# Hgrn stage: gate, query and forget products as three rounded passes, the residual spilled to memory, and the mixing stage moved to mLSTM's end

## The chip, the cores and the metric

One Trainium2 chip, of which the kernel uses one core. The metric is the device time of one execution in microseconds (us); a median of several runs stands for a kernel. All arrays are float32.

## The reference, cut to what matters

Three blocks run one after the other on a sequence of 512 tokens of width 1024. The change touches two places, both here in short.

```python
# first block, mixer of layer 0 (HGRN): h is the normed input, hc the normed context of 256 tokens
q, v, zf, zb, gate = split(h @ w_in, 5)          # w_in: 1024 x 10240, 16 heads of 128
f = lb + (1 - lb) * sigmoid(z)                   # for zf and zb; g = log f, k = 1 - f
# per head and direction, with the context's state before it:
#   S_t = diag(exp g_t) S_{t-1} + k_t^T v_t ;  o_t = S_t^T silu(q_t)
y = (rmsnorm(o_forward + o_backward) * silu(gate)) @ w_out
x = x + gate_ada * y

# second block, three mixers side by side:
#   mLSTM (4 heads); gmlp: gelu(u) * (tril(ws) @ layer_norm(gelu(v)) + bs), 4 groups, chunks of 128 tokens;
#   attention with compressed keys: 31 windows of 32 tokens, phi(k) = gelu((window + pe) @ phi1) @ phi2, the same for v
```

## The kernel before, in words

The program is a row of stages. Each stage is a block of its own: every engine has its own instruction list in it, semaphores order them, and all engines meet at its end. Activations lie transposed in SBUF, `[128 partitions, 8 slices of the width, 512 tokens]`: `K.xT` is the residual stream, `K.hT` the normed input of a stage, `K.ctxT` the normed context.

`modulation_phase` (L255) streams 72 MB of matrices through six buffers; its loads are all issued by SyncE's queue (SP), and a norm stage follows it.

`hgrn_phase` (L439) loops over 16 heads. For each head, SP loads five weight tiles of 1024 x 128 (`W[m]` for V, ZF, ZB, Q, G; each load waits for the last product that used its buffer). TensorE runs `project(h)`: eight products in the order of `GROUPS`, namely V over the 512 tokens and over the context (L542), then ZF and ZB each over the 512 tokens and over the 256 tokens of the context, then Q and G over the 512 tokens (L548). A float32 product appears in the trace as two MATMUL records, so 16 records make one product of 1024 x 128 x 512. The products rotate through four PSUM banks, so product n waits until product n-4 has been read out. After `project(h)` TensorE runs `recur(h-1)`, the scores and states of the head before. In the middle of `project(h)`'s V product stands `mean_square(h-2)` (L529), the sum for the norm of head h-2.

ScalarE (ACT) works in a fixed order, `step(h)`: the logarithms of the forget gates of head h-1 (`logs`, L645), the exponentials of its forward direction (`exps`, L653 to L659), the read-out of V of head h, the exponentials of the backward direction, the read-out of ZF, ZB, Q and G (sigmoid and silu, L637, L639), then `recur(h-1)`, which ends with Ln and Exp of the mean square (L670, L672); that last pair waits for TensorE's `mean_square`, one head later. VectorE (DVE) finishes head h-2 (L779, L782), scales the gates of head h-1 (`f1`, L717, and `kk`, L721), scans them (L728, L729), forms differences (L735 to L743), and, when the exponentials are there, the products with q and k (L754 to L758). GpSimd (POOL) is idle in the loop.

Elsewhere in the kernel the large products are already done in three rounded passes: ACT copies a weight tile to the type fp32r (the high part, `WH`), POOL subtracts it from the original (the low part, `WL`), and TensorE adds high x high, high x low and low x high, one MATMUL record each (`product_phase`, L797; POOL's subtraction is L845, ACT's copy L877, TensorE's passes L861 to L863; in later stages L1877 and L2826 are such subtractions).

`mlstm_phase` (L1285) computes four heads and, between them, 16 side products (L1343), of which the last four run at its end. Its last head's norm is two products with a matrix of ones (L1380 mean, L1382 square). The stage after it, `mix_compress_phase` (L1503), loads its weights with 14 DMAs, transposes the gmlp matrices, does the gmlp mixing (L1545, and L1546 for the bias, 16 of each), the window products over 31 windows (L1555, 128 of 64 x 64 x 31), the same products for the position (L1561, one column each), and a small second layer. Then `attention_phase` starts.

Of the kernel before, what the change touches and what calls it, by code (L numbers as in the profile page):

```python
# [83 lines left out]
def constants_phase(K):  # L84
# [15 lines left out]
    K.tri = K.sb(K.ctx, "tri", [P, P])  # L100
    K.xT = K.sb(K.ctx, "xT", [P, KD, T])
    K.hT = K.sb(K.ctx, "hT", [P, KD, T])
# [152 lines left out]
def modulation_phase(K):  # L255
# [9 lines left out]
    with ExitStack() as st:  # L265
# [7 lines left out]
        summed, copied, turned, biased, zeroed, ready = sems[SLOTS:SLOTS + 6]  # L273
# [12 lines left out]

# [152 lines left out]
def hgrn_phase(K, hO):  # L439
# [12 lines left out]
    with ExitStack() as st:  # L452
        W = [K.sb(st, f"hg_w{m}", [P, KD, P]) for m in range(5)]
        vt = [K.sb(st, f"hg_v{i}", [P, NT // P, P]) for i in range(2)]
        sg = [[K.sb(st, f"hg_sig{i}{d}", [P, NT]) for d in range(2)] for i in range(2)]
        qs = [K.sb(st, f"hg_q{i}", [P, T]) for i in range(2)]
        gs = [K.sb(st, f"hg_gate{i}", [P, T]) for i in range(2)]
        f1 = [K.sb(st, f"hg_f{d}", [P, NT]) for d in range(2)]
# [14 lines left out]
        osq = K.sb(st, "hg_osq", [P, T])  # L473
# [3 lines left out]
        tmp = K.sb(st, "hg_tmp", [P, 32])  # L477
        tmp2 = K.sb(st, "hg_tmp2", [P, 32])
# [5 lines left out]
         at_ok, kv_ok, s_ok, out_ok, sq_ok, ms_ok, ln_ok, rs_ok, o1_ok, fin_ok, back_ok) = sems[5:31]  # L484

# [10 lines left out]
        with nc.Block() as block:  # L496
            @block.sync
            def _(sp):
                clear_old(sp, old)

                def load(h, first, shift=0):
                    at = h * P if first else sp.snap(h * P)
                    for m in (V, ZF, ZB, Q, G):
                        if not first:
# [3 lines left out]
                with sp.Fori(0, NH - 1) as before:  # L508
                    load(before, False, P)

# [13 lines left out]

            @block.tensor
            def _(pe):
# [4 lines left out]
                def project(h, p, first=False, owed=None):  # L531
                    for n, (m, c) in enumerate(GROUPS):
                        if c == 0:
                            pe.wait_ge(w_in[m], 16 * h + 16)
                        if n >= 4 or not first:
# [10 lines left out]
                        else:  # L546
# [76 lines left out]
            def _(act):  # L623
                act.wait_ge(f_ok, 1)
                act.activation(tmp2[:, :], tmp[:, :], ACT.Exp).then_inc(g_ok, 1)

                def evacuate(h, p, groups):
                    for n in groups:
                        m, c = GROUPS[n]
                        act.wait_ge(proj, NG * h + (n + 1))  # L630
                        bank = ps[n % 4]
# [3 lines left out]
                        elif m in (ZF, ZB):  # L635
                            s = sg[p][m - ZF]
# [37 lines left out]
                def step(h, p):  # L674

                    logs(h - 1)
# [6 lines left out]
                evacuate(0, 0, range(NG))  # L683
# [10 lines left out]
            def _(dve):  # L694
# [3 lines left out]
                dve.tensor_tensor(tmp[:, :], x, x, ALU.subtract).then_inc(f_ok, 1)  # L698
                dve.wait_ge(g_ok, 1)
                dve.reciprocal(lb[:, :], tmp2[:, :]).then_inc(lb_ok, 1)  # L700
                dve.wait_ge(lb_ok, 1)
                dve.tensor_tensor(tmp[:, :], tmp2[:, :], lb[:, :], ALU.mult).then_inc(lb_ok, 1)
                dve.wait_ge(lb_ok, 2)
                dve.tensor_tensor(lb[:, :], tmp[:, :], tmp[:, :], ALU.subtract).then_inc(lb_ok, 1)
                dve.wait_ge(lb_ok, 3)
                dve.tensor_scalar(omlb[:, :], lb[:, :], -1.0, 1.0, ALU.mult, ALU.add).then_inc(lb_ok, 1)
                dve.memset(ones_c[:, :], 1.0).then_inc(f_ok, 1)
                dve.wait_ge(lb_ok, 4)
# [5 lines left out]
                def prepare(h, p):  # L714
                    for d in range(2):
                        dve.wait_ge(evac, NG * h + 4 + 2 * d)
                        dve.tensor_scalar(f1[d][:, :], sg[p][d][:, :], omlb[:, bass.ds(h + NH * d, 1)], TINY,  # L717
# [567 lines left out]
def mlstm_phase(K, qk, mv, so, gu, nq, kvc, ksw, gate_rows, Pt_room, room):  # L1285


    nc = K.nc
    BM, NM, IB = gate_rows
    w = K.inp["w_in_2"][0].rearrange("(k p) n -> p k n", p=P)  # L1290
    WS = 6
    side = [(((MO + i * P, P),), so, i) for i in range(4)] + [(((GU + i * P, P),), gu, i) for i in range(4)]
    side += [(((NQ + i * DH, DH), (NQ + (i + 4) * DH, DH)), nq, i) for i in range(4)]
    side += [(((NKC + i * P, P),), kvc, i) for i in range(2)] + [(((NKS + 2 * i * P, P),), ksw, i) for i in range(2)]
# [10 lines left out]
    with ExitStack() as st:  # L1305
        Pt = Pt_room[:, :, :].rearrange("q (b j) t -> q b j t", b=2)
        D, floor, h, sq, rs = room[:, 0:2, :], room[:, 2:4, :], room[:, 4:6, :], room[:, 6, :], room[:, 7, :]
        W = [K.sb(st, f"ml_w{s}", [P, KD, P]) for s in range(WS)]
        ps = K.psum_banks(st, "ml")
        SIDE_BANK = (ps[6], ps[7])  # L1310
        sems, old = K.phase()
# [4 lines left out]
        with nc.Block() as block:  # L1316
            @block.sync
            def _(sp):
                clear_old(sp, old)
                for n, (pieces, _, _) in enumerate(side):  # L1320
# [3 lines left out]
                    for at, width in pieces:  # L1324
                        sp.dma_start(W[n % WS][:, :, to:to + width], w[:, :, at:at + width]).then_inc(w_in[n % WS], 16)
                        to += width

            @block.tensor
            def _(pe):
# [46 lines left out]
                def norms(a):  # L1376
# [3 lines left out]
                    pe.matmul(ps[1][:, :], K.ones[:, :], h[:, a % 2, :], start=True, stop=True).then_inc(mean, 1)  # L1380
                    pe.wait_ge(sqd, a + 1)
                    pe.matmul(ps[1][:, :], K.ones[:, :], sq, start=True, stop=True).then_inc(var, 1)  # L1382

                for s in range(MH + 2):
# [6 lines left out]
                    if s >= 2:  # L1391
                        if s >= 3:
                            pe.wait_ge(ln_ok, s - 2)
                        norms(s - 2)

            @block.scalar
            def _(act):
# [32 lines left out]
                for s in range(MH + 2):  # L1430
# [9 lines left out]
                    if s >= 2:  # L1440
# [3 lines left out]
                        norms(s - 2)  # L1444

# [55 lines left out]


def mix_compress_phase(K, vn, gu, kvc, kcmp, vcmp):  # L1503


    nc, inp = K.nc, K.inp
    names = (("nsa_phi_k1_2", "nsa_phi_k2_2", "nsa_pe_k_2"), ("nsa_phi_v1_2", "nsa_phi_v2_2", "nsa_pe_v_2"))
    with ExitStack() as st:
        ws = K.sb(st, "gm_w", [P, 4, P])
        wT = K.sb(st, "gm_wT", [P, 4, P])  # L1510
        bs = K.sb(st, "gm_bias", [1, 4, P])
        w1 = [K.sb(st, f"cp_w1{n}", [P, 32, DH]) for n in range(2)]
# [1697 lines left out]
```

## Time and profile before

| | |
|---|---|
| median of 3 runs | 4458.1 us (4453.8 to 4460.87) |
| the profiled execution | 4456.16 us, span 4454.4 us |
| TensorE busy | 3947.5 us (89%) |
| VectorE / ScalarE / GpSimd busy | 40% / 28% / 13% |
| granted TensorE clock over the span | 0.93 of full |
| DMA | 313.34 MB, mean 70 GB/s, at most 387 GB/s in one of 40 slices |

The granted clock has two levels, full (2.4 GHz) and half (1.2 GHz); 0.93 is the mean. The hgrn stage lies at about 262 to 1281 us of the span, mLSTM at 2144 to 2318, the mixing stage at 2318 to 2377. The busy share of TensorE is that of whole stages with different limits, so the stages are read one by one.

### The profile page before, as it was taken

The page shows a single profiled execution, that of the slowest core. Times are in us where ns is not written, and L with a number is a line of the kernel's source. Part 1 is how long each engine was busy: PE and PEld are TensorE (multiplying, and loading weights), DVE is VectorE, ACT ScalarE, POOL GpSimd, SP SyncE. Part 2 cuts the span into 40 slices and gives each one's busy share as a digit, 9 for nine tenths or more (in the row PEclk, how much of TensorE's full clock was granted, in tenths as well). Part 3 has the DMA queues.
Part 4 walks back from the last instruction along what each step waited for, and adds up shares of the span by engine and source line. Part 5 has one row for each costly group of instructions (what it writes and reads, how often), then busy time and mean ns, then how long its engine had stood idle before and what let it go on. Part 6 is the DMA issues. An engine that isn't in the chain of part 4 may idle for free. (4 is left out here: it accounts for less than half of the span.)

```text
span 4454.4 us, 57808 instructions
## 1 busy us (share of the span) xinstructions
PE 3947.5 (89%) x23667; PEld 2612.2 (59%) x23667; DVE 1795.5 (40%) x2993; ACT 1237.7 (28%) x2102; POOL 576.5 (13%) x302
## 2 busy tenths in 40 slices
PE   5789999999968997877889999999786777899998
PEld 2356666666655443334446554788555657687876
DVE  1023445444441999312222333433226537334421
ACT  0133343333332111222212322332323131323321
POOL 0000000000011000001000001344330020243442
PEclk7789999999979999988987999999898888999999
DMA  8921111111023221011221103333120010232331
GB/s 314 387 64 44 47 42 42 40 40 47 24 57 94 76 73 60 19 53 38 61 37 48 43 24 104 85 96 99 33 54 2 13 46 3 77 95 85 95 90 62
DMA packets 484578, 313.34 MB, mean 70 GB/s; under 512 B 28364, under 2 KB 441605, under 8 KB 484390
## 3 DMA queue, kind: packets, MB, share of 16 engines
q1 hardware_dynamic: 484390, 310.67, 23.5%
q8 instruction: 137, 2.24, 0.2%
q14 instruction: 51, 0.42, 0.0%
HBM read 308.54 MB, written 2.10 MB: 70 GB/s over the span
## 5 line engine op out<-in xcount | busy, mean ns | idle before, releaser
L548 PE MATMUL hg_bank<-hT,hg_w 128*128 128x512 f32 x1024 | 447.3, 592 | 0.0
L1009 PE MATMUL cv_bank<-hT,cv_w 128*128 128x512 f32 x768 | 334.0, 596 | 14.2 <-DMA cv_w<-in_conv_w_in_dram 14.2
L548 PEld LDWEIGHTS hg_bank<-hT,hg_w 128*128 128x128 f32 x1024 | 193.5, 190 | 223.5 <-issue 221.8
L1083 DVE SCALAR_TENSOR_TENSOR conv_u<-cv_pad,vec,conv_u 128x512 f32<-128x512 f32 x480 | 318.7, 748 | 0.0
L2826 POOL TENSOR_TENSOR tl_wl<-tl_w,tl_wh 128x1024 fp32r<-128x1024 f32 (+1 forms) x104 | 246.4, 2371 | 520.0 <-ACT tl_wh L2937 519.9
L1009 PEld LDWEIGHTS cv_bank<-hT,cv_w 128*128 128x128 f32 x768 | 146.9, 191 | 199.6 <-issue 184.6
L1877 POOL TENSOR_TENSOR mp_wl<-mp_w,mp_wh 128x1024 fp32r<-128x1024 f32 x72 | 173.3, 2409 | 598.7 <-ACT mp_wh L1957 598.7
L2937 ACT ACTIVATE tl_wh<-tl_w 128x1024 fp32r<-128x1024 f32 (+1 forms) x104 | 108.5, 1043 | 357.5 <-PE tl_bank L2863 355.3
L2861 PE MATMUL tl_bank<-tl_room,tl_wh 128*128 128x512 f32 x464 | 186.2, 401 | 12.8 <-POOL tl_wl L2826 12.0
L2863 PE MATMUL tl_bank<-tl_room,tl_wl 128*128 128x512 f32 x464 | 183.8, 396 | 0.0
L2862 PE MATMUL tl_bank<-tl_room,tl_wh 128*128 128x512 f32 x464 | 182.7, 394 | 0.0
L1665 PE MATMUL at_bank<-hT,at_w 128*128 128x512 f32 x384 | 176.7, 604 | 0.3 <-DMA at_w<-in_w_in_dram 0.3
L845 POOL TENSOR_TENSOR ho_wl<-ho_w,ho_wh 128x2048 fp32r<-128x2048 f32 x8 | 36.6, 4580 | 1070.9 <-ACT ho_wh L877 1070.9
L763 DVE COPY hg_probe<-hg_bank 128x1 f32<-128x1 f32 x32 | 5.1, 159 | 397.6 <-PE hg_bank L563 397.6
L1957 ACT ACTIVATE mp_wh<-mp_w 128x1024 fp32r<-128x1024 f32 x72 | 76.2, 1060 | 252.2 <-PE mp_bank L1897 244.5
L2861 PE MATMUL tl_bank<-tl_hh,tl_wh 128*128 128x512 f32 x352 | 139.4, 396 | 4.3 <-DVE tl_rest L3041 4.3
L2863 PE MATMUL tl_bank<-tl_hh,tl_wl 128*128 128x512 f32 x352 | 139.5, 396 | 0.0
L2862 PE MATMUL tl_bank<-tl_rest,tl_wh 128*128 128x512 f32 x352 | 139.3, 396 | 0.0
L542 PE MATMUL hg_bank<-hg_w,hT 128*128 128x128 f32 x1024 | 121.5, 278 | 16.4 <-DMA hg_w<-in_hgrn_w_in_dram 16.4
L542 PEld LDWEIGHTS hg_bank<-hg_w,hT 128*128 128x128 f32 x1024 | 119.5, 194 | 24.6 <-DMA hg_w<-in_hgrn_w_in_dram 16.8
L1895 PE MATMUL mp_bank<-mp_dh,mp_wh 128*128 128x512 f32 x320 | 129.0, 403 | 0.0
L1897 PE MATMUL mp_bank<-mp_dh,mp_wl 128*128 128x512 f32 x320 | 124.7, 390 | 0.0
(657 smaller groups left out, 7713.1 us busy)
## 6 DMA issues: line engine op xcount, KB each, us to landing
ada_w<-in_w_ada_dram SPq DMA_DIRECT2D x24, 2048.0 KB, 19.7
hg_w<-in_hgrn_w_in_dram SPq DMA_DIRECT2D x80, 512.0 KB, 3.8
mp_w<-in_w_mlp_dram SPq DMA_DIRECT2D x64, 512.0 KB, 4.1
ada_w<-in_ada_w_dram SPq DMA_DIRECT2D x12, 2048.0 KB, 19.9
cv_w<-in_conv_w_in_dram SPq DMA_DIRECT2D x48, 512.0 KB, 3.9
tl_w<-in_w_ffn_in_dram SPq DMA_DIRECT2D x44, 512.0 KB, 3.9
at_w<-in_w_in_dram SPq DMA_DIRECT2D x24, 512.0 KB, 4.0
tl_w<-in_w_in_dram SPq DMA_DIRECT2D x20, 512.0 KB, 3.9
```

What stands on the lines that cost most here:

```text
L542: ins = pe.matmul(bank[:, t * P:(t + 1) * P], src[:, k, t * P:(t + 1) * P], W[m][:, k, :], start=(k == 0), stop=(k == KD - 1))
L548: ins = pe.matmul(bank[:, 0:w], W[m][:, k, :], src[:, k, 0:w], start=(k == 0), stop=(k == KD - 1))
L1009: ins = pe.matmul(ps[n % RING][:, :], W[n % SLOTS][:, k * P:(k + 1) * P], K.hT[:, k, :], start=(k == 0), stop=(k == KD - 1))
L1083: ins = dve.scalar_tensor_tensor(o, x, by, o, ALU.mult, ALU.add)
L1665: ins = pe.matmul(SIDE_BANK[:, :], W[n % WS][:, k, :], K.hT[:, k, :], start=(k == 0), stop=(k == KD - 1))
L1877: pool.tensor_tensor(WL[u % SPLIT][:, :, :], W[(UPS + u) % RAW][:, :, :], WH[u % SPLIT][:, :, :].bitcast(F32), ALU.subtract).then_inc(low, 1)
L1895: pe.matmul(bank[:, :], wh[:, k, :], rh[:, k, :], start=(k == 0), stop=False)
L1897: ins = pe.matmul(bank[:, :], wl[:, k, :], rh[:, k, :], start=False, stop=(k == KD - 1))
L2826: pool.tensor_tensor(WL[u % SPLIT][:, 0:n, :], W[u % RAW][:, 0:n, :], WH[u % SPLIT][:, 0:n, :].bitcast(F32), ALU.subtract).then_inc(low, 1)
L2861: pe.matmul(to[:, :], wh[:, wk, :], rh[:, k, :], start=first, stop=False)
L2862: pe.matmul(to[:, :], wh[:, wk, :], rl[:, k, :], start=False, stop=False)
L2863: ins = pe.matmul(to[:, :], wl[:, wk, :], rh[:, k, :], start=False, stop=last)
```

## The change

Six things are changed.

1. In the hgrn stage the products of ZF, ZB, Q and G over the 512 tokens become three rounded passes. ACT makes `WH` and POOL makes `WL` for each of the four weight tiles of each head; there are two buffers of each, ZF and Q share one, ZB and G the other. V and the products over the context stay as they were.
2. The rounded input `hh` and its rest `hl` are made once at the stage's start (8 ACT copies, 8 DVE subtractions).
3. To make room, `hh` lies where the residual `K.xT` lay: SP writes `K.xT` (2 MB) to memory at the end of the modulation stage and waits for it, and reads it back in the last head.
4. Q and G share one weight buffer: G's load waits for the split of Q, and Q's load of the next head for the split of G.
5. Sigmoid's result goes straight into `f1`, scaled in place, and some small tiles share room (the square `osq` lies on `ATS`).
6. `mix_compress_phase` is dissolved into `mlstm_phase`: its loads stand behind the first six side loads, its window products between the last head's mean and square, the rest behind; the bias of the mixing is one product of 512 columns for each group instead of four of 128. The side products change order (the four query ones last).

```diff
 @@ modulation_phase, sync
+                sp.dma_start(K.spill, K.xT[:, :, :].rearrange("p k t -> p (k t)")).then_inc(spilled, 16)
+                sp.wait_ge(spilled, 16)
 @@ hgrn_phase
-        W = [K.sb(st, f"hg_w{m}", [P, KD, P]) for m in range(5)]
+        W = [K.sb(st, f"hg_w{m}", [P, KD, P]) for m in range(4)]
+        W.append(W[Q])
+        WH = [K.sb(st, f"hg_wh{m}", [P, KD, P], F32R) for m in range(2)]
+        WL = [K.sb(st, f"hg_wl{m}", [P, KD, P], F32R) for m in range(2)]
 @@ sync, load(h, first): h + 1 is loaded
                     for m in (V, ZF, ZB, Q, G):
-                        if not first:
+                        if m == G:
+                            sp.wait_ge(low, 3 if first else 4 * h + 7)
+                        elif m == Q and not first:
+                            sp.wait_ge(low, 4 * h + 4)
+                        elif not first:
                             sp.wait_ge(proj, NG * h + LAST_OF[m])
...
+                sp.wait_ge(proj, NG * NH)
+                sp.dma_start(K.xT[:, :, :].rearrange("p k t -> p (k t)"), K.spill).then_inc(x_back, 16)
+                sp.wait_ge(x_back, 16)
 @@ gpsimd
+                with pool.Fori(0, NH) as h:
+                    for j, m in enumerate((ZF, ZB, Q, G)):
+                        pool.wait_ge(high, 4 * h + (j + 1))
+                        pool.tensor_tensor(WL[j % 2][:, :, :], W[m][:, :, :], WH[j % 2][:, :, :].bitcast(F32), ALU.subtract).then_inc(low, 1)
 @@ tensor, project
-                        if c == 0:
+                        if m == V and c == 0:
                             pe.wait_ge(w_in[m], 16 * h + 16)
+                        elif c == 0:
+                            pe.wait_ge(low, 4 * h + m)
...
+                        else:
+                            wh, wl = WH[(m - 1) % 2], WL[(m - 1) % 2]
+                            for k in range(KD):
+                                pe.matmul(bank[:, :], wh[:, k, :], hh[:, k, :], start=(k == 0), stop=False)
+                                pe.matmul(bank[:, :], wh[:, k, :], hl[:, k, :], start=False, stop=False)
+                                ins = pe.matmul(bank[:, :], wl[:, k, :], hh[:, k, :], start=False, stop=(k == KD - 1))
 @@ scalar
+                def weights_high(h, m, first=False):
+                    act.wait_ge(w_in[m], 16 * h + 16)
+                    if m in (Q, G):
+                        act.wait_ge(proj, NG * h + (3 if m == Q else 5))
+                    elif not first:
+                        act.wait_ge(proj, NG * h - (1 if m == ZF else 0))
+                    act.activation(WH[(m - 1) % 2][:, :, :], W[m][:, :, :], ACT.Copy).then_inc(high, 1)
 @@ scalar, evacuate: after the read-out of ZF and of ZB over the 512 tokens
+                        if m in (ZF, ZB) and c == 0:
+                            weights_high(h, Q if m == ZF else G)
 @@ scalar, step(h)
+                    weights_high(h, ZF)
+                    weights_high(h, ZB)
                     logs(h - 1)
                     exps(h - 1, 0)
                     evacuate(h, p, range(0, 2))
                     exps(h - 1, 1)
                     evacuate(h, p, range(2, NG))
                     recur(h - 1)
 @@ mlstm_phase, tensor, end
+                    if a == MH - 1:
+                        windows()
                     pe.wait_ge(sqd, a + 1)
                     pe.matmul(ps[1][:, :], K.ones[:, :], sq, start=True, stop=True).then_inc(var, 1)
...
+                def mixes():
+                    pe.wait_ge(wt_ok, 1)
+                    pe.wait_ge(hq, 4 * MH)
+                    for x in range(4):
+                        for c in range(TT):
+                            pe.matmul(MIX[x][:, c * P:(c + 1) * P], vn[:, c, x * P:(x + 1) * P], wT[:, x, :],
+                                      start=(c == 0), stop=False, skip_group_check=True)
+                        pe.matmul(MIX[x][:, :], K.ones[0:1, :], bs[:, x, :].unsqueeze(1).broadcast_to((1, TT, P)),
+                                  start=False, stop=True, skip_group_check=True).then_inc(mixed, 1)
...
+                positions()
+                mixes()
+                compressed()
```

`windows()` begins with the transposes, which wait for the stage's loads and for the last side product's read-out; `positions()` waits for DVE's copy of the transposed positions, which DVE does after the last head's norm.

## Rows read from the trace of the kernel before

**Rows 1.** Windows of the hgrn stage: busy us of each engine, clock, DMA.

```profile
480.00:540.00 60.00, 59.31 (x405) 40.85 (x405) 28.11 (x55) 22.95 (x43) 0.00 (x0) 1.00 0.15 43
```

**Rows 2.** Timeline of TensorE, one head: start us, us, engine, line.

```profile
682.12 3.74 PE L542 MATMUL hg_bank<-hg_w,hT 128*128 128x128 f32 x32
...
693.70 7.03 PE L548 MATMUL hg_bank<-hT,hg_w 128*128 128x512 f32 x16
700.57 3.62 PE L548 MATMUL hg_bank<-ctxT,hg_w 128*128 128x256 f32 x16
...
728.08 0.49 PE L582 MATMUL hg_bank<-ident,hg_ks 128*128 128x128 f32 x3
```

**Rows 3.** Timeline of TensorE with rounded passes, first and last of 14 triples.

```profile
1320.42 0.39 PE L861 MATMUL ho_bank<-ho_rh,ho_wh 128*128 128x512 f32 x1
...
1329.94 0.39 PE L861 MATMUL ho_bank<-ho_rh,ho_wh 128*128 128x512 f32 x1
```

**Rows 4.** Timeline of ScalarE, the same head as rows 2.

```profile
687.48 0.63 ACT L672 ACTIVATE hg_ors<-hg_ors 128x512 f32<-128x512 f32 x1
...
697.07 1.95 ACT L653 ACTIVATE hg_lev<-hg_lev 128x256 f32<-128x256 f32 x6 [4.92 <-DVE hg_ks L743]
...
701.45 0.85 ACT L634 ACTIVATE hg_v<-hg_bank 128x512 f32<-128x512 f32 x2
...
708.05 0.87 ACT L637 ACTIVATE hg_sig<-hg_bank 128x512 f32<-128x512 f32 x2
```

**Rows 5.** Timeline of VectorE, the same head.

```profile
689.65 1.14 DVE L717 TENSOR_SCALAR hg_f<-hg_sig,hg_omlb 128x768 f32<-128x768 f32 x2
```

**Rows 6.** Timeline where VectorE and GpSimd meet, two places.

```profile
2093.78 2.34 POOL L845 TENSOR_TENSOR qk_wl<-qk_w,qk_wh 128x1024 fp32r<-128x1024 f32 x1 [10.85 <-ACT qk_wh L877]
2094.57 1.83 DVE L1272 TENSOR_SCALAR merge_gate<-qk_pad,vec 128x512 f32 x1 [2.48 <-ACT qk_pad L1265]
...
2755.16 0.68 DVE L2047 TENSOR_TENSOR mp_dl<-merge_gate,mp_dh 128x512 fp32r<-128x512 f32 x1
2755.57 2.50 POOL L1877 TENSOR_TENSOR mp_wl<-mp_w,mp_wh 128x1024 fp32r<-128x1024 f32 x1 [374.86 <-ACT mp_wh L1957]
2755.77 2.85 DVE L2064 TENSOR_TENSOR merge_gate<-merge_gate 128x512 f32<-128x512 f32 x1
```

**Rows 7.** DMA issues: count, KB each, median us to landing (whole span; 2140 to 2150).

```profile
hg_w<-in_hgrn_w_in_dram SPq DMA_DIRECT2D x80, 512.0 KB, 3.8
ml_w<-in_w_in_dram SPq DMA_DIRECT2D x4, 512.0 KB, 6.2
```

**Rows 8.** Timeline: four loads issued in a row, and the first's reader.

```profile
2073.34 4.04 SPq L835 DMA_DIRECT2D qk_w<-in_w_in_dram  x4
2077.06 1.06 ACT L877 ACTIVATE qk_wh<-qk_w 128x1024 fp32r<-128x1024 f32 x1 [1.58 <-DMA qk_w<-in_w_in_dram]
```

**Rows 9.** Timeline of the modulation stage's end.

```profile
227.76 3.64 PE L314 MATMUL ada_bank<-ada_w,ada_cond 128*32 128x512 f32 x16 [0.90 <-DMA ada_w<-in_w_ada_dram]
...
235.62 1.28 ACT L394 ACT_TABLE_LOAD   x1 [3.56 <-PEq L274]
```

**Rows 10.** Timeline from mLSTM's last norm to the attention stage.

```profile
2311.18 1.02 PE L1380 MATMUL ml_bank<-merge_gate,ones 128*128 128x512 f32 x2
2313.70 1.13 PE L1382 MATMUL ml_bank<-merge_gate,ones 128*128 128x512 f32 x2 [1.50 <-ACT merge_gate L1423]
2317.04 0.69 DVE L1492 TENSOR_TENSOR ml_o<-ml_o,merge_gate 128x512 f32<-128x512 f32 x1
...
2324.49 0.80 PE L1545 MATMUL gm_bank<-gm_wT,gm_v 128*128 128x128 f32 x2 [0.78 <-DVE gm_wT L1583]
...
2347.80 13.87 PE L1555 MATMUL gm_bank<-nsa_kvc,cp_w 64*64 64x31 f32 x256
...
2377.61 0.76 PE L1678 MATMUL at_bank<-nsa_ksw,nsa_q 64*128 64x128 f32 x2 [0.80 <-PEq L1523]
```

**Rows 11.** Timeline of TensorE: small products at the full clock.

```profile
3459.79 6.87 PE L2615 MATMUL rw_bank<-rw_E 64*64 64x64 f32 x229
```

More of the change, by code:

```diff
@@ L100, in constants_phase @@
     K.tri = K.sb(K.ctx, "tri", [P, P])
+    with ExitStack() as under:
+        K.hgH = K.sb(under, "hg_hh", [P, KD, T], F32R)
     K.xT = K.sb(K.ctx, "xT", [P, KD, T])
+    K.spill = nc.dram_tensor("x_spill", [P, KD * T], F32, kind="Internal").ap()
     K.hT = K.sb(K.ctx, "hT", [P, KD, T])
@@ L484, in hgrn_phase @@
          at_ok, kv_ok, s_ok, out_ok, sq_ok, ms_ok, ln_ok, rs_ok, o1_ok, fin_ok, back_ok) = sems[5:31]
+        high, low, h_high, h_low, x_back = (K.ctx.enter_context(nc.semaphore(f"hg_sem{n}")) for n in range(5))
         GROUPS = [(V, 0), (V, 1), (ZF, 0), (ZF, 1), (ZB, 0), (ZB, 1), (Q, 0), (G, 0)]
@@ L545, in project @@
                                     mean_square(owed)
-                        else:
+                        elif c == 1:
                             for k in range(KD):
@@ L630, in evacuate @@
                         act.wait_ge(proj, NG * h + (n + 1))
+                        if n == 2 and not first:
+                            act.wait_ge(k_ok, 2 * h)
                         bank = ps[n % 4]
@@ L681, in step @@
                     recur(h - 1)
-                evacuate(0, 0, range(NG))
+                weights_high(0, ZF, True)
+                weights_high(0, ZB, True)
+                for k in range(KD):
+                    act.activation(hh[:, k, :], hT[:, k, :], ACT.Copy).then_inc(h_high, 1)
+                evacuate(0, 0, range(NG), True)
                 step(1, 1)
@@ new lines, in windows, with positions @@
+                def windows():
+                    turns()
+                    for x in range(2):
+                        for l in range(32):
+                            for r in halves:
+                                pe.matmul(HID[r, NCMP * x:NCMP * (x + 1)], w1[x][r, l, :], kvc[r, x, l:l + 16 * (NCMP - 1) + 1:16],
+                                          start=(x == 0 and l == 0), stop=(l == 31), skip_group_check=True)
+                def positions():
+                    pe.wait_ge(pos_ok, 1)
+                    for x in range(2):
+                        for l in range(32):
+                            for r in halves:
+                                ins = pe.matmul(HID[r, 2 * NCMP + x:2 * NCMP + x + 1], w1[x][r, l, :], peT[r, x, l:l + 1],
+                                                start=False, stop=(l == 31), skip_group_check=True)
+                    ins.then_inc(first, 1)
@@ L1384, in _, with compressed @@
+                def compressed():
+                    pe.wait_ge(hid, 2)
+                    for r in halves:
+                        pe.matmul(POS[r, 64:64 + NCMP], w2[0][r, :], h1[r, 0, :], start=True, stop=True)
+                    for x, r in enumerate(halves):
+                        ins = pe.matmul(SECOND[1 - x][0:NCMP, 128:128 + DH], h1[r, 1, :], w2[1][r, :], start=True, stop=True)
+                    ins.then_inc(second, 1)
                 for s in range(MH + 2):
@@ L1444, in _ @@
                         norms(s - 2)
+                for x in range(4):
+                    act.activation(gu[:, x, :], gu[:, x, :], ACT.Gelu_apprx_tanh).then_inc(gelu, 1)
+                act.wait_ge(bias_ok, 1)
+                for x in range(2):
+                    act.activation(h1[:, x, :], HID[:, NCMP * x:NCMP * (x + 1)], ACT.Gelu_apprx_tanh, bias=bias[:, x:x + 1]).then_inc(hid, 1)
             @block.gpsimd
```

167 lines of the change are left out of this document (66 added, 101 removed).

## The prediction, made before the changed kernel ran

> **What bounds the kernel now.** I read the page first, then the windows of the hgrn stage, then the timelines of its engines over one head, then the places where the three rounded passes already run, then the stretch from mLSTM's end to attention. In the hgrn stage TensorE is busy 59.3 of 60 us at the full clock [rows 1]: there it sets the time, so a shorter product is worth its whole saving as long as what feeds it keeps up. The other stretch is different: between mLSTM's last mean and the first attention product lie 66.4 us [rows 10], partly a wait for loads and partly small products.
>
> I count from the start of one head's projection (t = 0 is 682.12 in rows 2). V over tokens and context ends at 11.58, a product over 512 tokens takes 6.87, the projection ends at 45.96; so 45.96 - 11.58 - 4 x 6.87 = 6.9 is left for the two context products, 3.45 each. The rest of the head, 15.4 us, is untouched.
>
> **The product itself.** Rounded passes start every 9.52 / 14 / 3 = 0.227 us at the full clock [rows 3]. Eight slices times three passes take 5.44 us instead of 6.87: 1.43 saved, 5.72 a head, 91.5 over 16 heads if nothing else waits.
>
> **What feeds it.** ACT gets four copies a head of 1.06 us [rows 8], POOL four subtractions of 2.35 to 2.4 us [rows 6]. The question is whose work they delay.
>
> ACT is free at 5.99 (the end of Exp, 5.36 + 0.63) [rows 4]. Its two copies for ZF and ZB run to 8.05, and POOL subtracts from about 7.1 on, back to back. ZF's low part is ready near 9.9, before TensorE wants it at 11.58. But DVE starts the gates' scaling at 7.53 [rows 5] and works without a gap until the differences are done, when ACT begins the exponentials at 14.95 [rows 4]. Rows 6 show what happens when both engines want SBUF: a DVE operation of 512 columns met by a subtraction took 1.83 and 2.85 us and ended 0.3 and 0.55 us after POOL did; its neighbour that ran before took 0.68. A waiting POOL gets its turn after the DVE operation under way. The types are those of the gates' scaling (TENSOR_SCALAR) and the differences (TENSOR_TENSOR). So the 2 x 2.35 us are inserted into DVE's chain: I take +4.6 us for the start of the exponentials. If nothing blocked, the copies and the table load alone would delay it by about 0.8; those are the ends.
>
> The Trainium skill states this as a rule (SBUF — State Buffer, "Who interferes with whom"): a DVE instruction with two SBUF inputs, or in a two-port mode, and a GpSimd instruction that reads SBUF exclude each other for the whole instruction. By that rule the scans, which these rows do not show, block as well; the sum stays the same, since the subtractions then still cost 4.7 us in all. It is the rule that speaks against this change.
>
> From there with +4.6: exponentials start at 19.55, V is read out from 23.93 (19.33 before [rows 4]), the first of it is done near 24.5. ZB's product reuses V's bank. TensorE comes to it at 11.58 + 5.44 + 3.45 = 20.47 and now waits 4.1 us, where before it had room. ZB runs to 30.0, its context part to 33.45. The sigmoid of ZF starts at 25.93 + 4.6 = 30.53 [rows 4]; behind it the copy for Q runs 31.03 to 32.09; POOL, after the DVE operation under way (0.3), subtracts until 34.75; TensorE starts Q at 34.85, 1.4 late, and ends it at 40.3. Only now may SP issue G's load, at 34.9; behind it in the queue go V, ZF and ZB of the next head, all already allowed. A load alone lands after 3.8 us [rows 7], and the first of four in a row was used 3.7 us after its issue [rows 8]. I take 3.85: 38.75. ACT stands at that wait with its read-outs of ZB's context, Q and G queued behind; they keep, since no bank is needed for another 9 us. Copy to 39.85, subtraction to 42.3, G from 42.4 to 47.85. That is 1.9 us later than 45.96: **TensorE saves 5.7 us and waits 7.6**, and ACT's, POOL's and SP's chain sets the head. DVE's products with q and k end near 36.5 instead of 29.5, wanted at 47.8.
>
> Heads 0 and 1 differ. In head 0 nothing of an older head stands in ACT's way: -5.7. In head 1 the mean square is absent and the chain starts earlier against TensorE: V's bank is free in time, G waits about 0.5: -5.2. Heads 2 to 15: 14 x 1.9 = +26.6. **Hgrn: +15.7.** A TensorE wait of 4.1 us could drop the clock to half for a stretch. The slack left to TensorE before G is 3.5 us (1.4 + 2.1), about what 6.9 us at half clock lose, so I put it at nothing; without that slack it is 3 us in each head it strikes.
>
> **Costed at nothing.** The rounding of the input (8 short copies and subtractions) hides in head 0's V products, 12 us. Reading the residual back (2 MB) hides in the last two recurrences, 57 us. The spill queues behind the last modulation load, which has landed when its product starts at 227.76; the stage ends near 235.4 [rows 9], so 2 MB has 8 us. At the highest rate of the page, 387 GB/s, 2.1 MB take 5.4 us, so it fits; if not, or if it slows that load, up to +6. The 14 loads moved into mLSTM stand in SP's queue before the seventh side load, which TensorE wants only in the third head.
>
> **The mixing stage.** Now the order is mean (2311.2 to 2312.2), transposes (to 2312.9), windows, square, then 4.0 us of ACT and DVE (from 2313.70 to 2317.73 in rows 10) before the positions may start, since DVE copies them only after the norm, then the mixing. Windows and positions took 13.8 us each at half clock [rows 10], 0.054 a record; at the full clock records of this size start every 6.87 / 229 = 0.030 [rows 11]: 7.7. The mixing's 64 records took 0.36 each at half clock. 32 of them stay: 11.5 us, or 3.6 at the pace of L542 at full clock [rows 2], plus four bias products of 512 columns, 0.86 each full, 1.75 half.
> - All at full clock: 2312.9 + 7.7 + 1.1 + 4.0 + 7.7 + 7.1 + 1.3 (second layer) = 2341.8, against 2377.6: -35.8.
> - All at half: 2312.9 + 13.8 + 1.9 + 4.0 + 13.8 + 18.5 + 1.3 = 2366.2: -11.4.
> - I take windows at nearly full clock (9), the 4 us wait and the one-column positions dropping it (12.5), the mixing partly recovered (13.5): 2354.3. Between the ends, **-23**, because rows 11 show small products at the full clock but not with one column.
>
> **Sum.** +15.7 - 23 = -7.3 on the profiled execution's 4456.2, that is 4448.9; the median of the runs lies 1.9 above that execution: **4451 us**.
>
> **Rivals.**
> - *G's load lands late* (slower). The four loads share the 16 DMA engines; where four went together, the median landing was 6.2 us [rows 7]. Then each of 14 heads ends 2.35 us later: +33, **4484**. It decides for slower from a landing of about 5.0 us on (14 x 1.16 makes the sum +8.9). Against it: the first of four in rows 8.
> - *DVE is not held back* by POOL here: the exponentials start 0.8 us late instead of 4.6. Then Q waits 1.4, G starts at 38.5, the projection ends at 43.95, 2.0 earlier than before: 14 x -2.0 - 11.4 = -39, with -23: **4396**. For it: no row shows this stage's own operations meeting a subtraction. Against it: rows 6.
> - *The change does what the product says*, every feeder in time: -91.5 - 23: **4344**. The load of G behind the split of Q forbids it: split, load, copy and split again take 2.35 + 3.85 + 1.06 + 2.35 = 9.6 us.
> - *The mixing gives nearly nothing* (all at half clock, spill +6): 4451 + 11.6 + 6 = 4469; part of the likeliest case's width.
>
> **Chances.** The likeliest case 0.62, own range 4434 to 4470 (14 heads x 0.6 us, the mixing's ends, the spill); late load 0.16; DVE free 0.17; full gain 0.05. A measurement of this kernel tells about 0.2%, 9 us, from no change. The likeliest case splits 0.22 faster, 0.28 same, 0.12 slower. Together: faster 0.22 + 0.17 + 0.05 = 0.44, same 0.28, slower 0.28. The range takes in both neighbours and leaves out the full gain and half of the late load: 4390 to 4487.
>
> **What would show it.** In the changed kernel: L548's successor at 0.227 us a record; DVE's scaling at the head's start at about 2.9 us instead of 0.6; TensorE idle three times a head, some 4 us before ZB on ACT's read-out of V, 1.4 before Q and 2.1 before G on POOL's subtraction; ACT idle before the copy for G on a DMA; a head of 63.2 us instead of 61.3. Attention starting about 23 us sooner after mLSTM's last mean. It is wrong if DVE's operations keep their lengths, if G's load takes 5 us or more, if the clock drops inside the head, or if the mixing runs at one clock throughout.

## The result, and the profile after

The changed kernel takes 4514.6 us (median of 4 runs, 4508.4 to 4517.2) against 4456.6 for the kernel before: ratio 1.0123, interval 1.0111 to 1.0135, 1.2% slower. The prediction was 4451, range 4390 to 4487. The profiled execution has a span of 4506.7 us, 52.3 more than before.

First the windows of four heads in a row, each from its first V product to the next head's (us, then busy us and count of PE, PEld, DVE, ACT, POOL, then clock, DMA share, GB/s). The last row is the stretch that [rows 1] show of before.

```profile
564.64:632.81 68.17, 57.72 (x443) 48.23 (x441) 32.34 (x55) 28.63 (x49) 11.93 (x4) 0.97 0.15 39
632.81:699.83 67.02, 60.35 (x440) 50.85 (x441) 32.34 (x55) 24.96 (x45) 11.92 (x4) 0.92 0.15 40
699.83:767.89 68.06, 58.69 (x442) 48.94 (x441) 32.33 (x55) 28.72 (x49) 11.95 (x4) 0.94 0.14 39
767.89:837.16 69.27, 63.12 (x440) 53.24 (x441) 32.33 (x55) 24.97 (x45) 11.94 (x4) 0.88 0.14 39
...
480.00:540.00 60.00, 49.84 (x408) 42.22 (x407) 32.34 (x55) 23.54 (x43) 9.56 (x3) 0.97 0.07 20
```

These heads take 67 to 69 us where a head took 61.4 and 63.2 was forecast. TensorE, busy 59.3 of 60 us before, now idles 6 to 10 us a head. POOL is busy 11.9 us with four subtractions, 2.5 more than four of 2.35: the rows below show which one is long. The clock, 1.00 in [rows 1], is 0.88 to 0.97.

The timeline of TensorE over one head (start, us, line; the last brackets hold the idle time and what ended it) shows the three waits that were forecast, and a fourth that was not, where the next head begins:

```profile
564.64 3.74 PE L567 MATMUL hg_bank<-hg_w,hT 128*128 128x128 f32 x32
...
576.14 0.48 PE L578 MATMUL hg_bank<-hg_hh,hg_wh 128*128 128x512 f32 x1
...
581.49 0.39 PE L580 MATMUL hg_bank<-hg_hh,hg_wl 128*128 128x512 f32 x1
581.72 3.61 PE L573 MATMUL hg_bank<-ctxT,hg_w 128*128 128x256 f32 x16
588.82 0.50 PE L578 MATMUL hg_bank<-hg_hh,hg_wh 128*128 128x512 f32 x1 [3.49 <-ACT hg_v L675]
...
591.83 0.63 PE L580 MATMUL hg_bank<-hg_hh,hg_wl 128*128 128x512 f32 x1
...
600.66 0.49 PE L578 MATMUL hg_bank<-hg_hh,hg_wh 128*128 128x512 f32 x1 [1.03 <-POOL hg_wl L544]
...
608.32 0.49 PE L578 MATMUL hg_bank<-hg_hh,hg_wh 128*128 128x512 f32 x1 [1.89 <-POOL hg_wl L544]
...
628.40 1.06 PE L637 MATMUL hg_bank<-hg_cum,hg_S 128*128 128x128 f32 x8
632.81 5.46 PE L567 MATMUL hg_bank<-hg_w,hT 128*128 128x128 f32 x32 [3.35 <-issue]
```

The last row is V of head 6. TensorE stood 3.35 us for nothing that the profile shows ("issue"), and then took 5.46 us for 32 records that took 3.74 a head earlier. Head 6 is where TensorE's loop over pairs of heads turns. The groups of lines from 360 to 1240 us show these stops as the only idle time of V's line (19.9 us over six turns, 3.1 to 3.5 each), and above it the waits of L578:

```profile
L578 PE MATMUL hg_bank<-hg_hh,hg_wh 128*128 128x512 f32 x416 | 180.6, 434 | 81.1 <-ACT hg_v L675 45.3 <-POOL hg_wl L544 35.8
...
L567 PE MATMUL hg_bank<-hg_w,hT 128*128 128x128 f32 x832 | 104.8, 288 | 19.9 <-issue 19.9
```

The DMA view of the same stretch (packets, MB, share of 16 engines; below it the loads of the stage, with the median us to landing), the kernel after first, then the kernel before:

```profile
q8 instruction: 58, 0.95, 0.5%
...
hg_w<-in_hgrn_w_in_dram SPq DMA_DIRECT2D x65, 512.0 KB, 5.6
```

```profile
q8 instruction: 8, 0.13, 0.1%
```

Before, the instruction queue was silent once the loop ran (its 8 packets lie ahead of 504 us); now it brings a 16 KB block about 9 times in each pair of heads.

Of the other engines, in the same head (the rows that answer to [rows 4, 5, 8]):

```profile
572.16 5.36 DVE L769 TENSOR_SCALAR hg_f<-hg_f,hg_omlb 128x768 f32<-128x768 f32 x2
...
583.80 1.95 ACT L696 ACTIVATE hg_lev<-hg_lev 128x256 f32<-128x256 f32 x6 [5.19 <-DVE hg_ks L795]
...
588.18 0.86 ACT L675 ACTIVATE hg_v<-hg_bank 128x512 f32<-128x512 f32 x2
...
594.79 0.60 ACT L678 ACTIVATE hg_f<-hg_bank 128x512 f32<-128x512 f32 x1
595.29 1.05 ACT L664 ACTIVATE hg_wh<-hg_w 128x1024 fp32r<-128x1024 f32 x1
...
596.41 4.12 POOL L544 TENSOR_TENSOR hg_wl<-hg_w,hg_wh 128x1024 fp32r<-128x1024 f32 x1 [19.31 <-ACT hg_wh L664]
...
596.77 0.68 DVE L809 TENSOR_TENSOR hg_cum<-hg_cum,hg_q 128x512 f32<-128x512 f32 x1
597.38 0.95 DVE L810 TENSOR_TENSOR hg_ks<-hg_ks,hg_k 128x768 f32<-128x768 f32 x1
...
600.70 8.03 SPq L519 DMA_DIRECT2D hg_w<-in_hgrn_w_in_dram  x5
...
604.69 1.06 ACT L664 ACTIVATE hg_wh<-hg_w 128x1024 fp32r<-128x1024 f32 x1 [7.59 <-DMA hg_w<-in_hgrn_w_in_dram]
...
605.83 2.36 POOL L544 TENSOR_TENSOR hg_wl<-hg_w,hg_wh 128x1024 fp32r<-128x1024 f32 x1 [5.29 <-ACT hg_wh L664]
```

The scaling (L769) met POOL's subtractions as forecast. The subtraction for Q took 4.12 us instead of 2.35, because DVE's products (L806 to L810) were running and POOL did not get in between them: it ended 2.2 us after the last of them, about its own length. G's load landed 4.0 us after its issue (median over the heads 3.9, at most 5.0).

The mixing stretch after, for [rows 10]:

```profile
2387.19 1.02 PE L1455 MATMUL ml_bank<-merge_gate,ones 128*128 128x512 f32 x2
...
2388.82 7.66 PE L1478 MATMUL ml_bank<-nsa_kvc,cp_w 64*64 64x31 f32 x256
2396.41 1.12 PE L1459 MATMUL ml_bank<-merge_gate,ones 128*128 128x512 f32 x2
2401.22 13.21 PE L1486 MATMUL ml_bank<-cp_peT,cp_w 64*64 64x1 f32 x256 [3.68 <-DVE cp_peT L1638]
2414.36 2.08 PE L1495 MATMUL ml_bank<-gm_wT,gm_v 128*128 128x128 f32 x8
2416.36 2.07 PE L1497 MATMUL ml_bank<-gm_bias,ones 1*128 1x512 f32 x2
...
2431.97 0.76 PE L1730 MATMUL at_bank<-nsa_ksw,nsa_q 64*128 64x128 f32 x2 [0.81 <-PEq L1383]
```

From the mean to attention it takes 44.8 us instead of 66.4: -21.6 against -23 forecast. The modulation stage, spill included, ends at 233.56 (235.62 in [rows 9]). So nearly all of the miss lies in hgrn. From its first V product to the first copy of the next stage it took 1013.98 us (267.79 to 1281.77), now 1085.66 (267.23 to 1352.89): **+71.7, where +15.7 was forecast**.

### The profile page after: what moved, and what is told of

It reads as the page before. It is cut to its first block and busy times, and to the rows that moved or that the text cites. A ratio compares the mean times of both kernels' runs of the same rounds, so it can differ in the third digit from the quotient of the medians.

```text
span 4506.7 us, 59140 instructions
## 1 busy us (share of the span) xinstructions
PE 3899.6 (87%) x24155; PEld 2721.1 (60%) x24155; DVE 1866.4 (41%) x3001; ACT 1303.2 (29%) x2174; POOL 764.5 (17%) x366
## 5 line engine op out<-in xcount | busy, mean ns | idle before, releaser
L544 POOL TENSOR_TENSOR hg_wl<-hg_w,hg_wh 128x1024 fp32r<-128x1024 f32 x64 | 188.2, 2950 | 832.3 <-ACT hg_wh L664 832.3
L578 PE MATMUL hg_bank<-hg_hh,hg_wh 128*128 128x512 f32 x512 | 220.4, 430 | 89.2 <-ACT hg_v L675 48.7
L580 PE MATMUL hg_bank<-hg_hh,hg_wl 128*128 128x512 f32 x512 | 211.2, 413 | 0.0
L579 PE MATMUL hg_bank<-hg_hl,hg_wh 128*128 128x512 f32 x512 | 210.8, 412 | 0.0
L2912 PE MATMUL tl_bank<-tl_room,tl_wh 128*128 128x512 f32 x464 | 187.6, 404 | 13.3 <-POOL tl_wl L2877 12.5
L578 PEld LDWEIGHTS hg_bank<-hg_hh,hg_wh 128*128 128x128 f32 x512 | 103.3, 202 | 127.0 <-ACT hg_v L675 54.4
L567 PE MATMUL hg_bank<-hg_w,hT 128*128 128x128 f32 x1024 | 129.3, 289 | 36.5 <-issue 19.9
L567 PEld LDWEIGHTS hg_bank<-hg_w,hT 128*128 128x128 f32 x1024 | 127.2, 205 | 44.8 <-issue 27.7
L897 POOL TENSOR_TENSOR qk_wl<-qk_w,qk_wh 128x1024 fp32r<-128x1024 f32 x8 | 18.9, 2360 | 747.7 <-ACT qk_wh L929 747.7
```

The costliest lines, as they stand in the source:

```text
L544: pool.tensor_tensor(WL[j % 2][:, :, :], W[m][:, :, :], WH[j % 2][:, :, :].bitcast(F32), ALU.subtract).then_inc(low, 1)
L567: ins = pe.matmul(bank[:, t * P:(t + 1) * P], src[:, k, t * P:(t + 1) * P], W[m][:, k, :], start=(k == 0), stop=(k == KD - 1))
L578: pe.matmul(bank[:, :], wh[:, k, :], hh[:, k, :], start=(k == 0), stop=False)
L579: pe.matmul(bank[:, :], wh[:, k, :], hl[:, k, :], start=False, stop=False)
L580: ins = pe.matmul(bank[:, :], wl[:, k, :], hh[:, k, :], start=False, stop=(k == KD - 1))
L2912: pe.matmul(to[:, :], wh[:, wk, :], rh[:, k, :], start=first, stop=False)
```

## Which part costs: each half alone

The kernel before with part 6 alone:

```diff
 constants_phase, modulation_phase, hgrn_phase   # as in the kernel before
 mlstm_phase, second_block                       # as in the changed kernel
```

> The kernel before with part 6 of the change alone (the mixing at mLSTM's end), hgrn and the residual as before. If the two halves of the change add up: the stretch from mLSTM's last mean to attention 44.8 us instead of 66.4, -21.6 us, 4435. If its length hangs on the clock that the stage finds: anywhere from -11 to -36.

Measured: 4438.6 us against 4458.1, ratio 0.9954 (0.9941 to 0.9968), -19.5 us. The stretch took 45.4 us.

The changed kernel with parts 1 to 5 alone, the diff the other way round:

```diff
 constants_phase, modulation_phase, hgrn_phase   # as in the changed kernel
 mlstm_phase, mix_compress_phase, second_block   # as in the kernel before
```

> The changed kernel with the mixing stage as before (parts 1 to 5 of the change alone). If the parts add up: before + 72 for hgrn, and nothing from the mixing: 4530 to 4535. If something of the other stages' clock hangs on where mixing starts, some us from that.

Measured: 4533.2 against 4458.2, ratio 1.0162 (1.0147 to 1.0177), +75. The two parts add up (+75 - 19.5 = 55.5; together +58). The mixing does what was forecast; hgrn alone has to be explained.

## The stop at the loop's turn

My theory after the trace: the rounded passes made TensorE's loop body longer, it no longer stays loaded, and every turn waits for its code. A float32 product is two weight loads and two matmuls, a rounded pass and a transpose one of each. The windows of one turn, before and after, count them:

```profile
620.68:743.54 122.86, 121.48 (x817) 83.15 (x817) 56.25 (x110) 45.89 (x86) 0.00 (x0) 1.00 0.15 43
...
632.81:767.89 135.08, 119.04 (x880) 99.79 (x881) 64.67 (x110) 53.69 (x94) 23.88 (x8) 0.93 0.15 40
```

Without the record that reaches over a window's edge, and with one that is missing from the second, that is 816 matmuls and 816 weight loads before, 880 and 880 after. With 43 and 49 further instructions of that turn in the trace (registers, semaphores, the branch) it makes 1675 before and 1809 after.

```diff
-                with pe.Fori(1, NH // 2) as j:
+                for j in range(1, NH // 2):
                     project(2 * j, 0, owed=2 * j - 2)
```

> The changed kernel with TensorE's loop over pairs of heads written out, everything else alike. In the changed kernel's trace TensorE stands 3.45 us before V of heads 4, 6, 8, 10, 12 and 14, where its loop turns, waiting for nothing that the profile shows, and runs 14 us longer at half clock behind these stops; instruction loads went from none to about 9 in each turn. Theory A (the loop body no longer stays in TensorE's instruction memory, so every turn waits for code): written out there is no jump, the 6 stops and the slow stretches behind them go: -20.7 - 14 = -35 us against the changed kernel, about 4480. Theory B (the stop comes from something else at that place, ACT, a load or a semaphore): as the changed kernel, 4514.

Measured: 4476.4 us, ratio to before 1.0047 (1.0033 to 1.0060), 38 us less than the changed kernel; in the profiled executions hgrn is 30 us shorter (1055.4). No V product stood at a turn any more. Heads 3 to 9 and 11 to 14 took 64.4 to 64.7 us each, heads 2 and 10 66.2, at a clock of 0.92. Then the other direction, the longer body in the kernel before, without rounding:

```diff
+                        elif m in (Q, G):
+                            for x in range(2):
+                                for k in range(KD):
+                                    ins = pe.matmul(bank[:, x * TC:(x + 1) * TC], W[m][:, k, :], src[:, k, x * TC:(x + 1) * TC],
+                                                    start=(k == 0), stop=(k == KD - 1))
```

> The kernel before, with the Q and G products done as two halves of 256 columns: same arithmetic, same columns, but 32 more products in each turn of TensorE's loop, 128 instructions, about as many as the change adds. Theory A (code): each turn now loads its instructions again, V of the even heads starts 3.5 us late: +20 to +35 us, 4477 to 4492. Theory B: two products of 256 columns last as long as one of 512 (3.45 x 2 against 6.87), so +1 us, 4458.

Measured: 4487.9 us, ratio 1.0074 (1.0060 to 1.0087), +30. The groups of TensorE's lines and the DMA view of this kernel, 360 to 1100 us:

```profile
L542 PE MATMUL hg_bank<-hg_w,hT 128*128 128x128 f32 x768 | 94.5, 284 | 15.9 <-issue 15.9
```

```profile
q8 instruction: 51, 0.84, 0.5%
```

Same arithmetic, no POOL, no rounding, and the stop is there. The same with `elif m == G` only:

> The kernel before with G's product alone in two halves: 64 more instructions in each turn of TensorE's loop, half of what the kernel with both in halves adds. If the cost comes when a limit on the loop's size is passed and not with each instruction, the outcome is one of two: no more instruction loads in the loop and the time of before (4458), or about 8 loads a turn and the whole cost (about 4488). A cost in proportion would give 4473.

Measured: 4491.9 us, ratio 1.0073 (1.0061 to 1.0085), +35, with as many instruction loads (51). Half the added instructions cost as much as all: it is a limit, passed somewhere between 1675 and 1739 instructions, and not a price for each. Is it the length of the body, or where it lies? The same lines with `elif m in (Q, G) and isinstance(h, int)`, so in heads 0 and 1 alone:

> The kernel before with the Q and G products in halves for heads 0 and 1 alone, ahead of TensorE's loop: 128 more instructions run once, the loop's body is that of before, only its place in the code moves. If the body's own length decides whether it stays loaded: no loads in the loop, 4457. If it is the number of blocks of 16 KB that the body touches, and 64 instructions more in the body were too many because it then touches one block more: moved by half a block, the old body of 6.7 blocks touches 8 as well, it is loaded again in every turn, +25 to +35 us.

Measured: 4476.8 us, the median of runs from 4458.7 to 4495.6, ratio 1.0033 (1.0018 to 1.0048). Neither outcome: in the profiled execution two of the six turns stopped, the turn into head 4 and the one into head 8 (period of the head ahead 65.8 and 65.4 us), the others did not (61.4), and the DMA view of 360 to 1100 us counts 25 loads:

```profile
502.55 2.71 PE L542 MATMUL hg_bank<-hg_w,hT 128*128 128x128 f32 x11 [4.28 <-issue]
...
627.86 2.38 PE L542 MATMUL hg_bank<-hg_w,hT 128*128 128x128 f32 x19
```

(The 6.7 blocks of that expectation came from a count of about 1712 instructions; the trace's 1675 are 6.5.) The loop that did not change is at the edge once its code has moved. So the place counts as well as the length; why some turns reload and others not stays open. Last a control, the loop of the kernel before written out:

> The kernel before with TensorE's loop written out, nothing else. A control: in the kernel before a turn of the loop costs about 0.1 us (heads of 61.43 and 61.42 us in turn). If writing out helps only where turns stop for code: 4457, within 3 us. If it helps or costs by itself (straight code must be loaded all the time too): some other time, and the -38 us measured with the changed kernel are to be read against it.

Measured: 4464.4 us, ratio 1.0012 (1.0003 to 1.0021), +7 by the medians. Its heads take 61.33 us (61.42 before) and hgrn 0.5 us less; the +7 lie in later stages and were not traced further. Writing out gains nothing where no turn stops.

The Trainium skill (Runtime: NRT & Kernel Launch, "Instruction fetch mechanics") says that an engine's instruction memory is refilled in blocks of 16 KiB, 256 instructions, and that a taken branch waits for a load when its target is not in the current window of two pages. The runs agree with the size of a block (0.95 MB in 58 loads is 16.4 KB a load), and the stop goes with the branch. They do not agree with the two pages: the loop of before, 6.5 blocks long, turned without a load. The same section of the Trainium skill gives TensorE room for 2048 instructions; here 1739 already did not stay.

## POOL against VectorE

In the kernel with the loop written out a head still takes 64.65 us, 3.2 more than before, where +1.9 was forecast. I moved the copies, and with them the subtractions, to where DVE is idle or can't delay anything. First that for Q:

```diff
 @@ scalar, step(h)
                     evacuate(h, p, range(0, 2))
+                    weights_high(h, Q)
                     exps(h - 1, 1)
 @@ scalar, evacuate: the copy for Q behind ZF's read-out is left to head 0
```

> The changed kernel with ACT's copy for Q moved ahead of the second set of exponentials (after V's read-out) instead of behind ZF's sigmoid. Theory C (the chain copy Q, split Q, load G, copy G, split G sets the end of a head): Q's low part is there at about 28.5 us from the head's start instead of 36, G's at about 38, both before TensorE wants them; the waits of 1.0 and 1.8 us go, the projection takes 45.4 instead of 49.3: 14 x -3.9 = -55, about 4460. Rival D (the copy pushes the sigmoids 1.06 us back and POOL then meets DVE's products all the same, the wait only moves): -10 or less, 4505 to 4515.

Measured: 4450.8 us, 64 less than the changed kernel; ratio to before 0.9979 (0.9970 to 0.9988). Q's wait is gone in every head and G's in most. The theory of the chain holds. Then, with TensorE's loop written out, the copies of the next head's ZF and ZB ahead of time:

```diff
 @@ scalar, evacuate: behind Q's silu
+                        if m == Q and not last:
+                            weights_high(h + 1, ZF)
 @@ scalar, recur
                     for d in range(2):
+                        if d == 1 and ahead is not None:
+                            weights_high(ahead, ZB)
 @@ scalar, step(h)
-                    weights_high(h, ZF)
-                    weights_high(h, ZB)
                     logs(h - 1)
...
 @@ scalar, outside the loop: head 1's copy for ZB ahead of step(1), the last two heads written out
```

> The changed kernel with TensorE's loop written out and the copies (and so the subtractions) for ZF and ZB of the next head moved to the end of the head before, behind Q's silu and into the recurrence, where VectorE has nothing to do. Theory E (POOL's two subtractions hold the gates' scaling back by 4.2 us, that delays the exponentials, V's read-out and so TensorE before ZB): the scaling takes 0.57 us each again, the exponentials start near 15 us from the head's start instead of 19.2, the 3.5 us wait before ZB goes. Q's and G's chain then waits 2.5 and 2.1 us, the head takes 60.3 instead of 64.65: 14 x -4.4 = -61 against the unrolled kernel, about 4415. Rival: the wait before ZB has another cause (ScalarE's own order), 4470 to 4476.

Measured: 4423.0 us, ratio 0.9917 (0.9905 to 0.9930), 53 less than with the loop alone written out. Heads of 60.2 to 60.5 us, five of them 61.9 to 62.1; the wait before ZB is gone, and the ones before Q and G are 2.1 and 1.8 to 2.0 us (0.3 to 0.4 before G in five heads). Both moves together:

> As the kernel with the early splits for ZF and ZB, and with the copy for Q ahead of the second exponentials too. If the steps add up, no feeder is late: split of Q done near 27 us (TensorE wants it at 29.4), G's load lands near 31, its split is done near 34.7 (wanted at 34.85), the projection takes 40.4 us, 5.7 less than before: hgrn -85, mixing -20: 4352. If G's split comes 1 us late a head: 4366.

Measured: **4358.5 us, ratio 0.9772 (0.9760 to 0.9785), 99 us faster than the kernel before**. In the profile TensorE is busy almost throughout at the full clock again; two heads in a row (windows), and rows of DVE, ACT, POOL and SP in the first of them:

```profile
588.69:644.56 55.87, 55.17 (x443) 47.37 (x442) 29.56 (x55) 26.56 (x47) 12.93 (x4) 1.00 0.18 48
644.56:700.44 55.88, 55.19 (x443) 47.36 (x442) 29.55 (x55) 26.57 (x47) 12.94 (x4) 1.00 0.18 48
```

```profile
596.21 1.15 DVE L776 TENSOR_SCALAR hg_f<-hg_f,hg_omlb 128x768 f32<-128x768 f32 x2
...
603.63 1.95 ACT L699 ACTIVATE hg_lev<-hg_lev 128x256 f32<-128x256 f32 x6 [4.91 <-DVE hg_ks L802]
...
609.89 5.82 POOL L544 TENSOR_TENSOR hg_wl<-hg_w,hg_wh 128x1024 fp32r<-128x1024 f32 x1 [31.70 <-ACT hg_wh L664]
...
615.87 8.03 SPq L519 DMA_DIRECT2D hg_w<-in_hgrn_w_in_dram  x5
...
619.84 1.06 ACT L664 ACTIVATE hg_wh<-hg_w 128x1024 fp32r<-128x1024 f32 x1 [2.98 <-DMA hg_w<-in_hgrn_w_in_dram]
```

The scaling takes 1.15 us for two again, the exponentials start 14.9 us into the head. Q's subtraction now takes 5.82 us behind DVE's products, which costs nothing, because it ends at 27.0 and TensorE wants it at 29.4. A head of 55.87 is the full 5.5 us of the rounded passes. The same kernel with TensorE's loop kept:

> The same as the kernel with all three copies early, but with TensorE's loop kept. The price of the loop's turns in a kernel in which nothing else waits: 6 x 3.45 = 21 us at least, up to 35 with the stretches at half clock behind them, against the one written out; if ScalarE's, not TensorE's, chain sets the head here, less than 21.

Measured: 4381.2 us, ratio 0.9826 (0.9813 to 0.9838): 22.7 us for the six turns by the medians. In the profiled executions hgrn alone is 31.6 us longer (959.6 against 928.0), within the 21 to 35 expected; from the attention stage on that execution is 8.4 us shorter, which was not traced.

One more try cost time. On the kernel with the loop written out, POOL's subtraction in four pieces:

```diff
+                        for x in range(4):
+                            s = slice(2 * x, 2 * x + 2)
+                            ins = pool.tensor_tensor(WL[j % 2][:, s, :], W[m][:, s, :], WH[j % 2][:, s, :].bitcast(F32), ALU.subtract)
+                        ins.then_inc(low, 1)
```

> The changed kernel with TensorE's loop written out and each of POOL's subtractions cut into four of 256 columns. Where DVE's scaling of the gates met the two subtractions it ran only when POOL had ended one of them. Theory F (DVE gets in between two operations of POOL, but POOL not between DVE's while these follow without a pause): DVE's chain now loses some 0.6 to 1.2 us at the head's start instead of 4.2, the exponentials start near 16 us, TensorE's 3.5 us before ZB nearly go: -2 to -3 us a head, 4435 to 4450. POOL's low part of Q is as late as before. Rival: POOL keeps SBUF for its whole run of subtractions, or takes turns such that DVE's chain loses the same 4 us in all: as the unrolled kernel, 4476.

Measured: 4488.8 us, ratio 1.0060 (1.0047 to 1.0073), 12 slower than without the cut. The rival was right. The timeline shows both engines taking turns, piece by piece, and the exponentials hardly earlier: TensorE still waits 3.2 us before ZB.

```profile
640.22 9.04 POOL L546 TENSOR_TENSOR hg_wl<-hg_w,hg_wh 128x256 fp32r<-128x256 f32 x8 [29.65 <-ACT hg_wh L667]
...
640.73 2.09 DVE L772 TENSOR_SCALAR hg_f<-hg_f,hg_omlb 128x768 f32<-128x768 f32 x2
...
644.74 1.75 DVE L783 TENSOR_TENSOR_SCAN hg_cum<-hg_keep,hg_cum 128x512 f32<-128x512 f32 x1
...
664.58 2.51 POOL L546 TENSOR_TENSOR hg_wl<-hg_w,hg_wh 128x256 fp32r<-128x256 f32 x1 [15.33 <-ACT hg_wh L667]
```

The eight pieces take 9.0 us instead of 5.5, and DVE's scaling, scans (1.75 us, 1.21 where POOL is idle) and differences each wait for one of them. In the last row a piece that comes while DVE is in its row of products takes 2.51 us, about four times its length: it too waited to their end.

## Why the prediction was wrong, step by step

The scale is the head that starts at 564.64, and the +56 us by which hgrn missed (71.7 - 15.7). The medians missed by 63.6 us: beside hgrn's 56 the stretch between hgrn and mLSTM's last mean grew by 4.9 us, untraced, and the median lies 6.2 above the profiled execution where 1.9 was taken.

- **"The rest of the head, 15.4 us, is untouched": the step that failed.** It holds inside a pair of heads, not where the loop turns. TensorE stood 3.1 to 3.5 us at each of six turns: the heads ahead of them took 67.8 to 68.2 us, 20.5 us above six of 64.6. The heads behind them took 64.7 to 69.4, another 14 us, with the clock down to 0.88. Together 34; writing the loop out took 38 from the median and 30 from hgrn, where heads 2 and 10 then ran slower instead. Without the stops the kernel takes 4476.4 us, inside the range: this term alone put the result outside it. I had costed what the new passes execute, and not that they lengthen the code. No count of the body's instructions stands in the prediction, and none of its rivals has this mechanism.
- **"POOL, after the DVE operation under way (0.3), subtracts until 34.75": wrong.** It ended at 35.9 (600.53), having waited for the whole row of products, about 1.8 us. DVE's products, which nothing cut into, ended at 33.7 and not near 36.5. The rule came from the second place of [rows 6], where a subtraction that began during one DVE operation (L2047) had its turn right behind it and took 2.50 us. There the next DVE operation (L2064) stands behind a semaphore wait in the code, while the products L806 to L810 of one direction have none between them; whether that makes the difference was not tested. Q started at 36.0 instead of 34.85 and everything behind it moved: the projection ended 49.3 us into the head, not 47.85. That is 1.4 us in each of 14 heads, +20.
- **The product**: right. From its start to the context product behind it 5.6 us (576.14 to 581.72), 5.44 forecast. The two starts of [rows 3] lie 14 triples apart, so the 0.227 us a record was read rightly.
- **The start of the exponentials**: 19.2 us (583.80), 19.55 forecast, by the mechanism named; the kernels with the splits for ZF and ZB ahead, where it returns to 14.9, show it by undoing it. The rule that the prediction took from the Trainium skill (SBUF — State Buffer, "Who interferes with whom"), that the two exclude each other for a whole instruction, agrees with that, and the scans do block too (1.75 us). The last shows in the kernel with POOL's subtractions in pieces. V's read-out began at 23.5 and TensorE waited 3.5 us before ZB, 4.1 forecast.
- **G's load** landed after 4.0 us, 3.85 forecast; over the heads the median is 3.9, and one took 5.0. The rival of a late load is out for this load, although the median of all of this stage's loads rose to 5.6 us: it is the three behind G's that are slow (medians 5.5 to 7.4), and nothing waits for them.
- **The clock.** Behind the wait before ZB it fell to half (0.63 us a record at 591.83, 0.39 elsewhere), and as forecast the slack before Q swallowed that, although the prediction also named a drop inside the head as a sign against itself. I had put the clock at 3 us "in each head it strikes" without slack: at the turns there is none.
- **Heads 0 and 1** took 4.8 and 3.4 us less than before, 5.7 and 5.2 forecast: +2.7.
- **The mixing** gave 21.6 of 23. Windows 7.7 us (9 forecast), positions 13.2 (12.5), the mixing 16.0 at half clock throughout (13.5; the price at half had been put at 18.5, but eight of its records took 2.1 us there, not 2.9); the wait between, 3.7 us instead of 4.0.
- **Spill and reload** cost nothing that the trace shows.

Sum: 34 + 20 + 2.7 = 56.7, against a miss of 56. The two rivals that I gave 0.17 and 0.05, DVE not held back and the full gain, are not what this order of work gives, but with the copies moved and the loop written out the full gain was there: -86 us in hgrn (928.02 instead of 1013.98), -91.5 by that rival. "The load of G behind the split of Q forbids it" was a statement on one order of ACT's list only.

## What to carry to other kernels

Count the instructions that an edit adds to a loop body, not only their time. A loop which stayed loaded can start to stop at each turn, by 3.1 to 3.5 us in the changed kernel and more where the clock falls behind the stop; the instruction queue in the DMA view shows it, and writing the loop out removes it. Where two engines hold each other off SBUF, move the work to where the other is idle or where the delay is covered; cutting it into pieces only made them alternate here.

## What the runs showed of the hardware that I had not expected

- TensorE's loop of 1675 instructions stays loaded, one of 1739 does not, and the same loop moved by 128 instructions stays in some turns (runs from 4458.7 to 4495.6 us).
- A POOL subtraction that begins while DVE is in its row of products waits for the end of the row (4.12, 5.82 and, for a piece of a quarter, 2.51 us). One that follows another of POOL's gets its turn after one DVE operation, and so did the one in [rows 6] (2.50 us). What makes the difference was not found.
- Straight code of about the same size, loaded once from end to end (40 blocks in 740 us), never made TensorE wait in hgrn.
